# Dilated attention heads taken two at a time in a two-block transformer kernel

## The reference, cut to what matters

```python
DILATED_PATTERNS = ((128, 1), (512, 4), (2048, 16))
# per 128-query block, for each (window, dilation):
idx = t[:, None] - dilation * jnp.arange(n_keys)[None, :]     # keys t, t-d, ...
s = jnp.where(idx >= 0, einsum('bhqd,bhqjd->bhqj', q_blk * scale, k_g), -inf)
lse = logsumexp(s); p = exp(s - lse); outs.append(einsum(p, v_g)); lses.append(lse)
...
mix = softmax(stack(lses), axis=0)
out = sum(mix[..., None] * stack(outs), axis=0)
```

## Time and profile before

| | us |
|---|---|
| median of 3 runs | 1205.48 (1205.0 to 1205.62) |
| profiled execution | 1204.71 |
| its span, first to last instruction | 1202.9 |
| PE busy | 1179.3 (98%) |
| DVE busy | 739.3 (61%) |
| ACT busy | 570.9 (47%) |

### The profile page before, as it was taken

The page is one execution under the profiler, slowest core; times in us unless marked ns, Lnnn a source line. Parts: engine busy times, 40 slices in busy tenths (PEclk is TensorE's granted clock), DMA queues, the critical chain, the costliest instruction groups (busy, mean ns, idle before and its releaser), DMA issues.

```text
span 1202.9 us, 18032 instructions
## 1 busy us (share of the span) xinstructions
PE 1179.3 (98%) x7560; PEld 1047.9 (87%) x7560; DVE 739.3 (61%) x990; ACT 570.9 (47%) x656; POOL 25.9 (2%) x35
## 2 busy tenths in 40 slices
PE   6999999999999999999999999999999999999997
PEld 5978998998999988888998998899987788878895
DVE  4866656668555556675765667655456745765575
ACT  5454445433544434454445533444434455745563
POOL 0000000001000000000000001000000000000000
PEclk9999999999999999999999999999999999999999
DMA  8754545556666453744545556866554643446320
GB/s 287 252 172 155 176 145 180 200 176 191 230 210 198 167 196 118 259 150 140 175 144 173 175 178 206 263 186 200 193 193 144 214 150 106 141 165 211 106 71 35
DMA packets 129823, 211.44 MB, mean 176 GB/s; under 512 B 6480, under 2 KB 52560, under 8 KB 129616
## 3 DMA queue, kind: packets, MB, share of 16 engines
q1 hardware_dynamic: 126944, 202.96, 50.7%
q0 software_dynamic: 1744, 6.29, 1.8%
q10 hardware_dynamic: 1056, 1.05, 0.2%
HBM read 209.24 MB, written 1.05 MB: 175 GB/s over the span
## 4 chain that ended last, share of the span: by engine, by line
PE 93%; DVE 3%; ACT 3%; issue 1%; DMA 0%; POOL 0%; DVEq 0%; POOLq 0%; ACTq 0%
PE ps L432 89%; PE ps L621 1%; ACT wh L894 1%; PE ps L755 1%; PE ps L656 1%; DMA hml<-in_xT 0%; PE ps L604 0%; PE ps L563 0%; ACT sg L1057 0%; ACT xh L930 0%; DVE sg L1589 0%; DVE wl L1315 0%; PE ps L738 0%; PE ps L628 0%; DVE yl L1778 0%
## 5 line engine op out<-in xcount | busy, mean ns | idle before, releaser
L1315 DVE TENSOR_TENSOR wl<-raw,wh 128x2048 fp32r<-128x2048 f32 (+2 forms) x195 | 429.0, 2206 | 186.7 <-ACT wh L894 186.3
L894 ACT ACTIVATE wh<-raw 128x2048 fp32r<-128x2048 f32 (+2 forms) x195 | 363.8, 1873 | 180.0 <-PE ps L432 172.5
L432 PE MATMUL ps<-xh,wh 128*128 128x256 f32 (+1 forms) x1200 | 338.1, 282 | 0.0
L432 PE MATMUL ps<-xl,wh 128*128 128x256 f32 (+1 forms) x1200 | 332.4, 277 | 0.0
L432 PE MATMUL ps<-xh,wl 128*128 128x256 f32 (+1 forms) x1200 | 332.4, 277 | 0.0
L432 PEld LDWEIGHTS ps<-xh,wh 128*128 128x128 f32 (+1 forms) x1200 | 224.2, 187 | 4.7 <-issue 3.4
L432 PEld LDWEIGHTS ps<-xl,wh 128*128 128x128 f32 (+1 forms) x1200 | 224.2, 187 | 0.9
L432 PEld LDWEIGHTS ps<-xh,wl 128*128 128x128 f32 (+1 forms) x1200 | 223.8, 187 | 0.4
L432 PE MATMUL ps<-wh,xh 128*128 128x512 f32 (+1 forms) x512 | 204.5, 399 | 13.8 <-DVE wl L1315 11.6
L432 PE MATMUL ps<-wl,xh 128*128 128x512 f32 (+1 forms) x512 | 197.3, 385 | 0.0
L432 PE MATMUL ps<-wh,xl 128*128 128x512 f32 (+1 forms) x512 | 197.2, 385 | 0.0
(11 more groups left out here) (243 smaller groups left out, 1381.3 us busy)
## 6 DMA issues: line engine op xcount, KB each, us to landing
raw<-in_w_in SPq DMA_DIRECT2D x91, 1024.0 KB, 5.0
raw<-in_w_gate_up SPq DMA_DIRECT2D x88, 512.0 KB, 4.9
raw<-in_w_down SPq DMA_DIRECT2D x20, 1024.0 KB, 5.0
raw<-in_w_out SPq DMA_DIRECT2D x16, 1024.0 KB, 4.9
raw<-in_w_proj_ret SPq DMA_DIRECT2D x8, 1024.0 KB, 4.9
raw<-in_w_proj_mlstm SPq DMA_DIRECT2D x8, 1024.0 KB, 5.0
rows<-in_ln_g POOLq DMA_DIRECT2D x4, 512.0 KB, 4.1
rows<-in_ln_b POOLq DMA_DIRECT2D x4, 512.0 KB, 5.8
```

The lines of the kernel that those rows point to most:

```text
L432: return pe.matmul(o, a, b, start=start, stop=False, skip_group_check=True)
L894: act.activation(stretch(wh, u, 0, m), raw[u % RAW][:, 0:m], ACT.Copy).then_inc(s_hi, 1)
L1315: dve.tensor_tensor(stretch(wl, u, a, nk * n), raw[u % RAW][:, a:nk * n], f32(stretch(wh, u, a, nk * n)), ALU.subtract).then_inc(s_lo, 1 i ...
```

## The change

A step now takes a pair of heads. `S 0` makes the scores of heads 0 and 1, and so on; `N`, `T` and `V` likewise. The slots that held one step of each kind hold a step of one or two kinds, and the order of the PSUM tiles follows. Scores and probabilities go through four tiles (`tp[h % 4]`); the transposed ones take `tp[4]` and a part of `lr[0]`, a tile of the LRU. The number and the shape of the instructions stay as they were, but for the reciprocals, of which there are half as many, each on four columns instead of two.

```diff
-AUX2 = ("r00", "r01", "r10", "r11", "S0", "S1", "S2", "T0", "S3", "T1", "V0", "S4", "T2", "S5", "T3", "V1", "S6", "T4", "S7", "T5",
-        "V2", "T6", "c0", "c1", "T7", "V3", "c2", "c3", "l0", "l1", "k0", "k1", "k2", "k3", "p0", "p1",
+AUX2 = ("r00", "r01", "r10", "r11", "S0", "S1", "S2", "S3", "T0", "T1", "S4", "S5", "V0", "T2", "T3", "S6", "S7", "V1", "T4", "T5",
+        "V2", "c0", "c1", "T6", "T7", "c2", "c3", "V3", "l0", "l1", "k0", "k1", "k2", "k3", "p0", "p1",
...
-    "ag": (("S 0",), ("S 1", "N 0"), ("S 2", "N 1", "T 0"), ("ag0", "S 3", "N 2", "T 1", "V 0")),
-    "cqk": (("ag1", "S 4", "N 3", "T 2", "V 1"), ("S 5", "N 4", "T 3", "V 2"), ("S 6", "N 5", "T 4", "V 3"),
-            ("S 7", "N 6", "T 5", "V 4")),
-    "b": (("N 7", "T 6", "V 5", "sc 0"), ("T 7", "V 6", "se 0", "sc 1"), ("V 7", "se 1"), ("b0", "sl")),
+    "ag": (("S 0",), ("N 0",), ("S 1",), ("N 1", "ag0", "T 0")),
+    "cqk": (("S 2", "ag1", "V 0"), ("N 2", "T 1"), ("S 3", "V 1"), ("N 3", "T 2")),
+    "b": (("V 2", "sc 0"), ("T 3", "se 0", "sc 1"), ("V 3", "se 1"), ("b0", "sl")),
...
+        probT = tp[4][:, 0:384], lr[0][:, :, :].rearrange("p k t -> p (k t)")[:, 0:384]
...
+            def dil_scores(l, pr):
...
+                for hh in range(2):
+                    bank, fill = open_aux(f"2S{2 * pr + hh}", l)
+                    q_, k_ = qkT[64 * hh:64 * hh + 64, pr, :], qkT[64 * hh:64 * hh + 64, 4 + pr, :]
+                    mm(bank[:, 0:P], q_[:, 0:P], k_[:, 0:P], True)
+                    mm(bank[:, P:P + S], q_[:, P:S], k_[:, :], False).then_inc(fill, 1)
+
+            def dil_turn(l, pr):
+                for h in (2 * pr, 2 * pr + 1):
+                    bank, fill = open_aux(f"2T{h}", l)
+                    pe.wait_ge(s_prob, 8 * l + h + 1)
+                    for a in (0, P, S):
+                        r = pe.transpose(bank[:, a:a + P], tp[h % 4][:, a:a + P], ident)
+                    r.then_inc(fill, 1)
+
+            def dil_values(l, pr):
+                bank, fill = open_aux(f"2V{pr}", l)
...
+                for hh in range(2):
+                    h, p0 = 2 * pr + hh, 64 * hh
+                    aux_done(f"2T{h}", l)
+                    mm(bank[p0:p0 + 64, 0:S], av[:, 0, 64 * h:64 * h + 64], probT[hh][:, 0:S], True)
+                    r = mm(bank[p0:p0 + 64, P:S], av[:, 1, 64 * h:64 * h + 64], probT[hh][:, S:S + P], False)
+                r.then_inc(fill, 1)
...
-            def dil_prob(l, h):
-                dve.wait_ge(s_den, 8 * l + h + 1)
-                after(own(dve.reciprocal(dden[:, 2 * h:2 * h + 2], dden[:, 2 * h:2 * h + 2])))
...
+            def dil_prob(l, pr):
+                dve.wait_ge(s_den, 8 * l + 2 * pr + 2)
+                after(own(dve.reciprocal(dden[:, 4 * pr:4 * pr + 4], dden[:, 4 * pr:4 * pr + 4])))
+                for h in (2 * pr, 2 * pr + 1):
...
+                    r.then_inc(s_prob, 1)
```

More of the change, by code:

```diff
@@ L739, in rope_turn @@
                     r.then_inc(fill, 1)
-            def dil_scores(l, h):
-                bank, fill = open_aux(f"2S{h}", l)
-                if h == 0:
+            def dil_scores(l, pr):
+                if pr == 0:
                     for name in ("2r00", "2r01", "2r10", "2r11"):
                         aux_done(name, l)
[L746 to L762, removed]
+                for hh in range(2):
[3 more added lines that the diff above has]
+                    mm(bank[:, P:P + S], q_[:, P:S], k_[:, :], False).then_inc(fill, 1)
@@ L1155, in rope_turn, with dil_exp, dil_turn, dil_out @@
                     act.activation(qkT[:, 4 * c:4 * c + 4, tok_half(t)], bank[:, :].rearrange("p (g c) -> p g c", g=4), ACT.Copy).then_inc(drained, 1)
[L1157 to L1168, removed]
+            def dil_exp(l, pr):
+                for h in (2 * pr, 2 * pr + 1):
+                    _, _, drained, n = aux(f"2S{h}", l)
+                    act.wait_ge(drained, n + 1)
+                    for t, (a, z) in enumerate(spans):
+                        k = 2 * h + t
+                        r = act.activation(tp[h % 4][:, a:z], tp[h % 4][:, a:z], ACT.Exp, bias=dmin[:, k:k + 1], scale=-1.0,
+                                           accum_out=dden[:, k:k + 1])
+                    r.then_inc(s_den, 1)
+            def dil_turn(l, pr):
+                for hh in range(2):
+                    bank, fill, drained, n = aux(f"2T{2 * pr + hh}", l)
+                    act.wait_ge(fill, n + 1)
+                    act.activation(probT[hh], bank[:, 0:384], ACT.Copy).then_inc(drained, 1)
             def y_high(k):
                 act.activation(yh[:, k, :], sg2[:, k, :], ACT.Copy).then_inc(s_yh, 1)
[L1173 to L1177, removed]
+            def dil_out(l, pr):
+                _, _, drained, n = aux(f"2V{pr}", l)
+                act.wait_ge(drained, n + 1)
+                y_high(pr)
             def copy_av(l):
@@ L1758, in rope, with dil_scores @@
                 dve.tensor_tensor(x2, q4[2], q4[3], ALU.add).then_inc(s_rope, 1)
[L1760 to L1765, removed]
-            def dil_prob(l, h):
-                dve.wait_ge(s_den, 8 * l + h + 1)
-                after(own(dve.reciprocal(dden[:, 2 * h:2 * h + 2], dden[:, 2 * h:2 * h + 2])))
-                for t, (a, z) in enumerate(spans):
-                    r = dve.tensor_scalar(tp[h % 3][:, a:z], tp[h % 3][:, a:z], dden[:, 2 * h + t:2 * h + t + 1], None, ALU.mult)
-                r.then_inc(s_prob, 1)
+            def dil_scores(l, pr):
+                for h in (2 * pr, 2 * pr + 1):
+                    bank, drained = aux_full(f"2S{h}", l)
+                    for t, (a, z) in enumerate(spans):
+                        r = dve.tensor_tensor_reduce(tp[h % 4][:, a:z], bank[:, a:z], C("lnc", a, z), 1.0, 3.0e38, ALU.add, ALU.min,
+                                                     dmin[:, 2 * h + t:2 * h + t + 1])
+                    r.then_inc(drained, 1)
+            def dil_prob(l, pr):
+                dve.wait_ge(s_den, 8 * l + 2 * pr + 2)
+                after(own(dve.reciprocal(dden[:, 4 * pr:4 * pr + 4], dden[:, 4 * pr:4 * pr + 4])))
+                for h in (2 * pr, 2 * pr + 1):
+                    for t, (a, z) in enumerate(spans):
+                        r = dve.tensor_scalar(tp[h % 4][:, a:z], tp[h % 4][:, a:z], dden[:, 2 * h + t:2 * h + t + 1], None, ALU.mult)
+                    r.then_inc(s_prob, 1)
             def y_out(l, k, src, raised):
@@ L1778, in y_out, with dil_out @@
                 dve.tensor_tensor(yl[:, k, :], v, f32(yh[:, k, :]), ALU.subtract).then_inc(s_y, 1)
[L1780 to L1783, removed]
+            def dil_out(l, pr):
+                bank, drained = aux_full(f"2V{pr}", l)
+                y_out(l, pr, bank[:, 0:S], drained)
             def silu_end(l, name, b, k, n):
```

## The result

The changed kernel takes 1189.16 us (median of 4 runs, 1188.91 to 1190.04) against 1205.36 us of the kernel before: a ratio of 0.9868 with a 95% interval of 0.9856 to 0.9881, 16.2 us less. The profiled execution took 1189.2 us, its span 1187.4.

A forecast was written before the change was run, and what follows sets the result against it. PE, busy 98% of the span, was taken as the bound. Visits falling from 20.27 to 12.19 us gain 8.08 a layer, 16.2 in two, taking the median from 1205.48 to 1189.3 us; 8-in-10 range 1186.5 to 1193.

The forecast's parts named there:

- PE is the bound, without waits, in this stretch: Dilated attention, first `S` to end of `b`: PE busy all 50.60 us, so only shorter PE work gains.
- Two heads cost what one costs: Scores and values of a pair: 0.86 and 0.81 us for two heads, against 0.85 and 0.79 for one.
- The sum: PE's visits in one layer's dilated attention: 20.27 us before, 12.19 after, a gain of 8.08.
- The surcharge for `V` straight behind `S`: Values right after scores on PE: none taken; upper bound 0.8 us in all.
- DVE and ACT stay hidden: Dilated attention: their 29.2 and 27.4 us fit behind PE's 42.5 us, with no local wait expected.
- The slack at `V 2`: Tightest place, after `cqk`: ACT's copies finish about 1.1 us before PE comes to `V 2`.
- Given back later: Late in the layer, low part of `y` 1 us late per layer: 2 us lost, 1191.3 us; chance 0.07.
- the split of the gain: Per layer: 6.6 us from the overlapping second head, 1.5 from fewer ways in and out.
- the first rival: Pairs in `S` and `V` do not overlap: gain 3.0 us, 1202.5; chance 0.05 for one or both kinds.
- ways in and out: PE entering and leaving a visit among regular matmuls: 0.09 us in, 0.10 out; fewer of them save 1.5 a layer.

The follow-up runs named there:

- each part alone: Two kernels, each the kernel before with one change: values of a pair made together, 1198.97 us; scores of a pair made together, 1198.80 us.
- four row groups: Changed kernel with the four decay matmuls of an mLSTM layer in the first block issued in one visit, from four copies of the row maxima: 1183.64 us.

## Why the prediction was right

- *PE is the bound, without waits, in this stretch; only shorter PE work counts.* Shown: the window shrank with PE busy all of it, and 3.84 us more of ACT in it did nothing.
- *Two heads cost what one costs.* Shown in both directions: 0.86 and 0.80 us for two, 1.50 and 1.44 on one half, and each part alone gave its share. The Trainium skill, page "TensorEngine Tiling (Array Packing)", section Tiling Modes, says that different tiles can load and multiply in parallel. The trace of four row groups agrees, 0.64 us for eight instructions.
- *The sum.* 42.5 us a layer were forecast for the window, 42.70 measured; a gain of 8.08 against 7.86. That the whole gain came out at 16.2 us to the tenth is luck: the two windows give 15.7, and the other half microsecond is outside them. `T` of a pair took 0.57 and not 0.54, and 0.74 before `sc` and not 0.69 (1006.65 to 1007.39), together 0.14 us of the 0.22; the other 0.08 are spread over 264 regular steps.
- *The surcharge for `V` straight behind `S`.* None: `S` 0.87 (985.94 to 986.81), `V` 0.80.
- *DVE and ACT stay hidden.* Shown. The slack at `V 2` was 1.4 us, forecast at about 1.1; from the end of `N` to `T` the first layer of the changed kernel has 4.4 to 6.2 us, where 4.5 or more were forecast.
- *Given back later.* Not seen: PE's wait for `yl` is 1.1 us as before.
- *The term that was mis-sized* is the split of the gain, and with it the price of the first rival. The text put 6.6 us a layer to the overlap, the full price of a lone head, and 1.5 to ways in and out, and so gave 1202.5 us to a kernel without overlap. Measured, that kernel takes 1199.43 us: 5.29 and 2.57. A lone `S` takes 0.85, but a second head behind the first on the same half only 0.64 more (1.50 - 0.86); the other 0.21 are not paid again. The name of the 1.5 is off too: the visits fall only from eleven to ten, and in the prediction's own sum 1.2 of the 1.5 are the transposes, six together instead of three (3.54 us a layer before, 2.31 after). Measured, they went from 3.55 to 2.45. The forecast did not rest on this split, since it added whole visits.

## What to carry to other kernels

Where PE is busy all the time, price small matmuls from start to start and ask which of them leave rows or columns of PE unused: two that use different halves cost what one does if they stand side by side. On the same half, side by side, a second head cost 0.64 us here; in visits apart it cost its whole step, 0.85 or 0.79 us. A neighbour that already works in pairs (`sc` and `sp` here) gives the price before anything is built. The hidden engines then do the same work in less time, so look up the tightest way from a transpose through its copy to the next use; here 1.4 us were left.

## What the runs showed that was not expected

In the program, head 1's two matmuls of a `V` stand behind both of head 0's. In the trace of the changed kernel head 1's first instruction (986.82) starts 0.25 us before head 0's second (987.07): on different halves PE does not start these matmuls in program order, and the sentence ahead of the prediction that each engine works strictly in its own order does not hold for them. On the same half it does: there head 1 starts behind all four instructions of head 0 (first starts 988.51 and 987.81). That putting the two heads into alternating order changed next to nothing fits this. Only `V` shows it directly, since there the two heads have tiles of different names.
